# First MLP with ten pair groups and one plain group at its end, in place of eight and two

## The reference, cut to what matters

```python
# end of first_block
h = rms_norm(x, g_pre_mlp) * (1.0 + scale2) + shift2
f = jnp.square(jax.nn.relu(h @ w_fc1)) @ w_fc2        # 1024 -> 4096 -> 1024
x = x + gate2 * rms_norm(f, g_post_mlp)
# start of second_block
h = rmsnorm(x, attn_norm_g)
z = h @ w_in
```

## Time and profile before

| | |
|---|---|
| median of 3 runs | 2761.06 us (2756.93 to 2766.6) |
| the profiled execution | 2762.93 us; its span, first to last instruction, 2761.1 us |
| PE busy, share of the span | 97% |
| DVE, POOL, ACT busy | 66%, 46%, 38% |
| mean granted PE clock | 0.991 of full speed |

### The profile page before, as it was taken

How to read it: one execution, slowest core, us unless ns; L and a number is a source line. 1 busy time by engine, 2 the same in 40 slices (tenths; PEclk the granted TensorE clock), 3 DMA queues, 4 the chain that set the end, 5 groups by cost and what they waited for, 6 DMA issues and landing times.

```text
span 2761.1 us, 36980 instructions
## 1 busy us (share of the span) xinstructions
PE 2688.5 (97%) x14232; PEld 2146.1 (78%) x14232; DVE 1830.9 (66%) x2487; ACT 1042.8 (38%) x1705; POOL 1260.5 (46%) x774
## 2 busy tenths in 40 slices
PE   7999999999999999999999999999999999999998
PEld 4888888788888878886888566666887788888877
DVE  4853324657777776565999843798567677777763
ACT  5001114434444433455221456655114344444433
POOL 1433323454777754452232114010334677777773
PEclk9999999999999999999999999999999999999999
DMA  8541114343211224344133200000431112221123
GB/s 324 162 143 39 39 39 130 100 154 98 66 58 55 68 62 145 99 137 112 46 97 98 61 1 1 2 2 3 175 114 42 58 55 65 64 69 58 55 66 108
DMA packets 252697, 225.78 MB, mean 82 GB/s; under 512 B 24667, under 2 KB 220778, under 8 KB 252266
## 3 DMA queue, kind: packets, MB, share of 16 engines
q1 hardware_dynamic: 249498, 215.02, 25.0%
q10 hardware_dynamic: 3024, 8.39, 0.8%
HBM read 197.16 MB, written 25.17 MB: 81 GB/s over the span
## 4 chain that ended last, share of the span: by engine, by line
PE 85%; DVE 7%; ACT 3%; issue 3%; POOL 2%; DMA 0%; SPq 0%; ACTq 0%; DVEq 0%; POOLq 0%
PE PS L1479 21%; PE PS L1709 11%; PE PS L2075 9%; PE PS L2109 8%; PE PS L1758 5%; PE PS L1725 5%; PE PS L1775 5%; PE PS L2016 3%; PE PS L1463 3%; PE PS L1921 2%; PE PS L1983 2%; PE PS L2149 1%; DVE STEP L3852 1%; PE PS L1952 1%; PE PS L1891 1%
## 5 line engine op out<-in xcount | busy, mean ns | idle before, releaser
L1122 POOL TENSOR_TENSOR WLO<-RAW,WHI 128x1024 fp32r<-128x1024 f32 x113 | 272.8, 2414 | 471.9 <-ACT WHI L2259 471.8
L1109 POOL TENSOR_TENSOR WHI<-RAW,ZERO 128x1024 fp32r<-128x1024 f32 x46 | 91.5, 1989 | 494.0 <-PE PS L1479 238.2
L2259 ACT ACTIVATE WHI<-RAW 128x1024 fp32r<-128x1024 f32 x114 | 120.8, 1060 | 413.5 <-PE PS L1479 147.6
L1479 PE MATMUL PS<-H,WHI 128*128 128x512 f32 x864 | 271.1, 395 | 2.3 <-ACT CX L2187 1.2
L1479 PE MATMUL PS<-L,WHI 128*128 128x512 f32 x864 | 267.4, 391 | 0.0
L1479 PE MATMUL PS<-H,WLO 128*128 128x512 f32 x864 | 267.0, 390 | 0.0
L4063 DVE TENSOR_TENSOR X<-X,PS 128x1024 f32<-128x1024 f32 x182 | 214.6, 1213 | 4.9 <-PE PS L2109 3.3
L1336 POOL TENSOR_TENSOR QLO<-QRAW,QHI 128x512 fp32r<-128x512 f32 x116 | 171.7, 1481 | 80.9 <-ACT QHI L2724 80.7
L1709 PE MATMUL PS<-H,WHI 128*128 128x512 f32 x496 | 196.5, 396 | 1.4 <-DVE WLO L3344 0.6
L1709 PE MATMUL PS<-H,WLO 128*128 128x512 f32 x496 | 193.7, 391 | 0.0
L1709 PE MATMUL PS<-L,WHI 128*128 128x512 f32 x496 | 193.7, 390 | 0.0
(11 more groups left out here) (535 smaller groups left out, 6637.3 us busy)
## 6 DMA issues: line engine op xcount, KB each, us to landing
RAW<-w_fc SPq DMA_DIRECT2D x64, 512.0 KB, 4.0
RAW<-w_in SPq DMA_DIRECT2D x62, 512.0 KB, 3.8
DOWNRAW<-w_ff SPq DMA_DIRECT2D x81, 256.0 KB, 2.6
ADA<-w_ada SPq DMA_DIRECT2D x32, 512.0 KB, 5.3
QRAW<-w_ff SPq DMA_DIRECT2D x32, 512.0 KB, 4.0
RAW<-w_out SPq DMA_DIRECT2D x24, 512.0 KB, 3.8
DOWNRAW<-w_fc SPq DMA_DIRECT2D x40, 256.0 KB, 2.6
ADA_FIRST<-w_ada SPq DMA_DIRECT2D x16, 512.0 KB, 9.7
```

The source lines that it names most:

```text
L1122: nc.gpsimd.tensor_sub(WLO[w % 2][:, :], RAW[w % 2][:, :], WHI[w % 2][:, :].bitcast(F32)).then_inc(s_w, 1)
L1479: last = mm(bank(b + t), wt[:, k, :], half(a, (k + at) % KC, t), start=(k == 0 and n == 0), stop=(k == KC - 1 and n == 2))
```

## The change

`TAIL` becomes 1: ten pair groups, and then two blocks (group 7, half 0) and (group 7, half 1). The tiles of these blocks are called T0 to T15 from here on, T0 to T7 being the first block; T16 is the first tile of the projection. Around this:

- `back_sum` moves from the down tiles to the up tiles of the first block. ACT's copy for `back_sum(i)` stands at the end of ACT's step for the same tile i; it stood one step later than DVE's sum.
- Chain 2 runs beside the second block alone. Its stage 0 sums and spread stay ahead of the same matmuls (in T9), its stage 1 sums and spread move from the tenth tile of the chain to its seventh, T14, ahead of the second and sixth eighth of the tile.
- On DVE the order is written anew: the reciprocal of stage 0 behind the multiply and the low part of the first up tile, updates and accumulations in turn, the norms between the last two `half_sum`s.
- On ACT the squares of chain 2 are taken two for each tile from T10 to T13, the stage 1 root behind T13's, `H` behind T14 and T15, and all squares of `Y` for chain 3 behind T15.
- POOL writes its four chunks of `L` behind `WLO` of T16.
- The residual comes back in two parts: chunks 4 to 7 behind the `RAW` of T4, chunks 0 to 3 behind the `RAW` of T8.

```diff
--- before.py
+++ after.py
@@ -494,7 +494,7 @@
                     KC, 2 * KC, KC, KC)
         assert M1.w % 2 == 0
 
-        HEAD, TAIL = 2, 2
+        HEAD, TAIL = 2, 1
         BLOCKS1 = [(g, e) for e in range(2) for g in range(HEAD)]
         BLOCKS2 = [(g, e) for e in range(2) for g in range(GROUPS - TAIL, GROUPS)]
 
@@ -863,13 +863,15 @@
 
                             sp.wait_ge(c_xn, KC + k + 1)
                             sp.dma_start(xs[:, k * S:(k + 1) * S], chunk(X, k)).then_inc(s_xs, 16)
-                        k = 8 * n + i - 11
-                        if w0 == M1T.w and 0 <= k < KC:
-
-                            if k == 0:
+                        if w0 == M1T.w and 8 * n + i in (4, 8):
+
+                            if n == 0:
+                                sp.wait_ge(f_mm, done1(up_unit1(NG1 - 1, 2)))
+                                sp.wait_ge(s_xs, 16 + 16 * KC)
+                            else:
                                 sp.wait_ge(e_lo, TOKEN1_AT["back", 3])
-                                sp.wait_ge(s_xs, 16 + 16 * KC)
-                            sp.dma_start(chunk(X, k), xs[:, k * S:(k + 1) * S]).then_inc(s_xr, 16)
+                            for k in range(0 if n else 4, 4 if n else KC):
+                                sp.dma_start(chunk(X, k), xs[:, k * S:(k + 1) * S]).then_inc(s_xr, 16)
                         if w0 == M1.w and n == 2 and i == 0:
 
                             sp.wait_ge(c_lod, KC)
@@ -1260,16 +1262,15 @@
             down_sum1(g, 2)
             for n in range(4, 7):
                 down_low1(g, n)
-            for t in range(32):
-                if t == 29:
-                    chain_lows(2, 0)
-                if t == 30:
-                    chain_lows(2, 2)
+            for t in range(16 * TAIL):
                 low_part(M1T.w + t)
             for i in range(len(Z_TILES)):
                 if i == Z_OPEN:
                     chain_lows(3, 0)
                 low_part(Z0 + i)
+                if i == 0:
+                    chain_lows(2, 0)
+                    chain_lows(2, 2)
                 if i == Z_OPEN:
                     chain_lows(3, 2)
                 if i == Z_INDEX + 1:
@@ -1689,6 +1690,11 @@
                         chain_sums(q, 1)
                     if p == 5 and k == 6:
                         chain_spread(q, 1)
+                elif q == 2:
+                    if p == 6 and k == 1:
+                        chain_sums(q, 1)
+                    if p == 6 and k == 5:
+                        chain_spread(q, 1)
                 else:
                     if p == 9 and k == 2:
                         chain_sums(q, 1)
@@ -1782,13 +1788,13 @@
                 for n, (g, e) in enumerate(blocks):
                     for i in range(8):
                         t = 8 * n + i
-                        p = t - 16 * (q % 2 == 0)
+                        p = t - 8 * (m is M1T)
                         chain = q if 0 <= p < 16 else None
                         if i < 4:
                             ready = chain_ready(q - 1 + e) if i == 0 and n % 2 == 0 and m is M1 else None
                             if m is M1T and n == 0 and i == 1:
                                 pe.wait_ge(f_add, added1(NG1 - 1, 6) + 2)
-                            if m is M1T and n == 2 and i == 0:
+                            if m is M1T and n == 1 and i == 0:
                                 pe.wait_ge(e_lo, TOKEN1_AT["back", 3])
                             half_up(m.w + t, e, (H, L), ready, chain, p)
                         else:
@@ -2507,22 +2513,33 @@
                 act.wait_ge(f_mm, done1(ALONE1 + 4 + 2 * t))
                 high_part(M1T.w + t)
 
+            def sums_squared(n, columns):
+
+                for c in columns:
+                    act.wait_ge(*reads(M1T.w + 8 * n + 4 + c))
+                    for k in (2 * c, 2 * c + 1):
+                        branch_squared(16 + KC * n + k, half(Y, k, n))
+
             def tail_act(n, i):
 
-                e = n // 2
-                if n % 2 == 1 and i >= 5:
-                    for c in range(i - 5, i - 4 if i < 7 else 4):
-                        act.wait_ge(*reads(M1T.w + 8 * n + 4 + c))
-                        for k in (2 * c, 2 * c + 1):
-                            branch_squared(16 + KC * e + k, half(Y, k, e))
-                if n >= 2:
-                    chain_act_long(2, 8 * (n - 2) + i)
-                if n == 1 and i == 7:
-                    chain_act_long(2, -1)
-                if 5 <= 8 * n + i < 9:
-                    token_sum_high("back", 8 * n + i - 5)
-
-            half_blocks(M1T, BLOCKS2, 0, 34, tail_act)
+                if n == 0 and i >= 5:
+                    sums_squared(n, range(i - 5, i - 4 if i < 7 else 4))
+                if n == 0 and i < 4:
+                    token_sum_high("back", i)
+                if n == 0 and i == 7:
+                    chain_root(2, 0)
+                if n and 2 <= i <= 5:
+                    chain_square(2, 2 * i - 4)
+                    chain_square(2, 2 * i - 3)
+                if n and i == 5:
+                    chain_root(2, 1)
+                if n and i >= 6:
+                    for k in range(4 * i - 24, 4 * i - 20):
+                        chain_high(2, k)
+                if n and i == 7:
+                    sums_squared(n, range(4))
+
+            half_blocks(M1T, BLOCKS2, 0, 16 * TAIL + 2, tail_act)
             chain_act_short(3, -1)
 
 
@@ -3323,14 +3340,14 @@
 
             def hidden_low(m, n, i):
 
-                e, u = n // 2, 4 * n + i
+                e, u = n // (HEAD if m is M1 else TAIL), 4 * n + i
                 dve.wait_ge(*reads(m.w + 8 * n + i))
                 dve.wait_ge(s_hi, m.hi + u + 1)
                 V.tensor_sub(half(FL, i, e), RL[i % 2][:, HALF:S], half(FH, i, e).bitcast(F32)).then_inc(s_lo, 1)
 
             def half_sum(m, n, c, first=False):
 
-                e, w = n // 2, m.w + 8 * n + 4 + c
+                e, w = n // (HEAD if m is M1 else TAIL), m.w + 8 * n + 4 + c
                 dst = chunk(Y, 2 * c, 2).rearrange("p (c s) -> p c s", c=2)[:, :, e * HALF:(e + 1) * HALF]
                 src = bank(w_bank(w), 2).rearrange("p (c s) -> p c s", c=2)
                 dve.wait_ge(s_mm, w + 1)
@@ -3558,10 +3575,10 @@
 
             def back_beside(i):
 
-                if i >= 4:
-                    if i > 4:
-                        back_low(i - 5)
-                    back_sum(i - 4)
+                if 1 <= i <= 4:
+                    back_low(i - 1)
+                if i < 4:
+                    back_sum(i)
 
             def twelve_begun1(g):
 
@@ -3689,11 +3706,33 @@
             for n in range(4, 7):
                 down_read1(g, n)
             dve.wait_ge(f_add, added1(g, 6) + 2)
-            plain_block(M1T, 0, beside=back_beside)
-            plain_block(M1T, 1, squares=16, beside=lambda i: back_low(3) if i == 0 else None)
+            plain_block(M1T, 0, squares=16, beside=back_beside)
             dve.wait_ge(s_xr, 32 * KC)
-            chain_long(2, M1T, 2, False)
-            plain_sums(M1T, 3, squares=24)
+            for i in range(4):
+                hidden_squared(M1T, 1, i)
+                hidden_low(M1T, 1, i)
+                if i == 0:
+                    chain_recip(2, 0)
+                chain_update(2, i)
+                if i:
+                    chain_added(2, i)
+            chain_update(2, 4)
+            chain_added(2, 4)
+            half_sum(M1T, 1, 0)
+            chain_update(2, 5)
+            chain_added(2, 5)
+            half_sum(M1T, 1, 1)
+            chain_update(2, 6)
+            chain_added(2, 6)
+            chain_update(2, 7)
+            chain_added(2, 7)
+            chain_recip(2, 1)
+            chain_norms(2, 0, 3)
+            half_sum(M1T, 1, 2)
+            chain_norms(2, 4, 8)
+            half_sum(M1T, 1, 3)
+            for k in range(KC):
+                branch_square(24 + k)
             chain_recip(3, 0)
             chain_steps(3, 0, 9)
             chain_recip(3, 1)
```

## The result

The changed kernel takes 2779.59 us (median of 5 runs, 2777.13 to 2782.22), the kernel before 2761.06 us (now of 5 runs, the same median): ratio 1.0068, 95% interval 1.0057 to 1.008. It is slower, as forecast, by 18.5 us where 13 were forecast, and just above the range. The profiled execution took 2781.57 us (span 2779.8), 18.6 more than that of before.

What follows compares the result with a forecast made beforehand. PE's queue was taken to bound the kernel: waits of 22.7 us less 11.5 gained, net +11.2, plus 1.5 for the clock, +12.7; 2774 us after adjusting from the profiled execution to the runs' median, range 2764 to 2779.

Steps and rivals of the forecast that it cites:

- what PE gains: Two blocks of 88.1 us go out of PE's queue, two pair groups of 76.6 us come in: gain 11.5 us.
- RS in T9: PE waits 2.4 us at the stage 0 spread, the reciprocal being queued behind T8's multiply and `FL`.
- XACC in T14: PE waits 8.6 us at the stage 1 sums for DVE's last accumulations; floor of the term 6.3.
- the five places in T16 and T17: DVE's norms, ACT's `H` and POOL's `L` come late; 0.4 to 0.5 us lost at each place, 2.2 together.
- the circle: T10 to T14: one chain 2 update and accumulation, over DVE and ACT, takes about 2.9 us with the semaphores.
- the fetches: Residual chunks go out four together, twice, with `RAW` of T5 and T9 queued behind: costed at nothing, from above 4 us.
- The forecast's other case: First block: if POOL does not hold DVE's adds, the same walk gives a net 2.8 us lower.
- the walk to +6.6: First block: `back_sum` ends about +6.6 us after ACT's `WHI` starts, from `FL`'s end at 4.08 plus 2.5.
- Rival 4: The fetches late as well: net +15 to +19 us, 2776 to 2780; chance 0.06.
- I take one, after the longest, 1.5: Clock term: one half-clock stretch, after the longest wait, costs PE 1.5 us, making the net +12.7.
- rival 3: Half clock after every long wait, four over 2 us: 11.2 + 6 = +17.2 us, 2778; chance 0.14.
- Rival 1: Volume decides, not order: chain 2 hides in the blocks, whole 11.5 us gained, 2749.6 us; chance 0.09.

Runs made afterwards that it cites:

- run 1: Changed kernel with ACT's copy for `back_sum` one step later, as before the change: 2772.22 us, ratio 1.005 to the kernel before.
- run 2: Changed kernel with the stage 0 reciprocal ahead of T8's multiply and low part on DVE: 2774.82 us, ratio 1.0057 to the kernel before.
- run 4: Changed kernel with chain 2's stage 1 sums and spread in T15 in place of T14: 2772.1 us, ratio 1.0053 to the kernel before.
- run 5: Changed kernel with the squares of the first four chunks of `Y` and their additions taken early: 2773.44 us, ratio 1.005 to the kernel before.
- run 3: Changed kernel with 72 unread filler matmuls in the waits of T4, T9, T14 and T17: 2768.32 us, ratio 1.0038 to the kernel before.
- run 6: Changed kernel with the four order edits of runs 1, 2, 4 and 5 together: 2760.25 us, ratio 1.0005 to the kernel before.
- run 7: Run 6 reordered further: DVE's updates and accumulations earlier, five ACT squares a tile earlier, stage 1 sums back in T14: 2757.89 us, ratio 0.9995.
- run 9: Run 7 with unread filler matmuls, 10 ahead of the sums in T14 and 7 ahead of those in T17: 2752.83 us, ratio 0.9975.
- run 8: The changed kernel itself, unedited, measured again beside runs 5, 6 and 7: 2777.41 us, ratio 1.0062 to the kernel before.
- run 10: Changed kernel with 36 unread filler matmuls in the XACC wait of T14 alone: 2774.36 us, ratio 1.0052 to the kernel before.

## Why the prediction was off in size

**Right: what PE gains.** The two pair groups took 76.9 us, forecast 76.6. The first block took 50.2 us, forecast 48 to 50; 1.6 of it is clock.

**Right: the waits.** Forecast and measured, in us: `WLO` for T4 1.5 and 1.05; `FL` in T4 3.6 and 3.26; RS in T9 2.4 and 2.23; `FL` in T12 0.7 and 0.84; XACC in T14 8.6 and 8.23; the five places in T16 and T17 2.2 and 1.1; YACC in T17 3.3 and 3.67. ACT's steps beside T1 to T3, forecast 6.6, 7.2 and 7.2 us apart, were 6.55, 7.15 and 7.11, each ending in the copy that waits for DVE:

```profile
1106.14 1.05 ACT L2265 ACTIVATE WHI<-RAW 128x1024 fp32r<-128x1024 f32 x1
...
1112.79 0.60 ACT L2375 ACTIVATE H<-PS 128x512 fp32r<-128x512 f32 x1 [4.45 <-DVE PS L3521]
1113.29 1.05 ACT L2265 ACTIVATE WHI<-RAW 128x1024 fp32r<-128x1024 f32 x1
```

Runs 1, 2, 4 and 5 each took one cause away and its wait went, wholly or by the part forecast from its place. In the circle two accumulations came 2.74 us apart, where 2.9 was taken.

**Right in part by luck: their sum.** Without the clock the forecast's net is +11.2, and the account gives 20.5 - 9.2 = 11.3. But the waits were 19.6 us where the forecast added up 21.8, and the restarts and short gaps about 3 where it had 0.9. Two errors of 2 us cancel. A restart costs more than the 0.1 that the forecast took: around the 3.26 us wait in T4 two matmuls start 3.65 us apart (1120.83 and 1124.48), which is 3.26 + 0.23 and 0.16 more, and the next one follows after 0.33 us in place of 0.23.

**Right: the fetches are hidden.** The eight took 4.5 to 8.2 us to land (4.5/6.5/8.2, against the earlier trace rows), longer than any before, and no wait of the stage names them. The adds of `back_sum` were not held by POOL in T1 to T3: they took 0.68 to 0.69 us, because `WLO` was over by then; `FL` took 1.72 to 1.77 beside it. So the port rule of the Trainium skill ("SBUF — State Buffer", "SBUF: two separate sides") agrees with `FL`, and had no part in the adds here. The forecast's other case, a net 2.8 us lower if the adds are not held, did not come with it: the walk to +6.6 had already taken them at 0.6 us apart, as not held. Rival 4 (2776 to 2780) holds the measured time by its number only, since the fetches delayed nothing.

**Wrong: the clock.** The step that failed is "I take one, after the longest, 1.5". It had two faults. The count: not one stretch but four, one behind each wait of over 2 us, which is rival 3's mechanism. The size: rival 3 priced each at 1.5, "from above 6 us", and so this bound was no bound. The stretch behind the 8.2 us wait cost 3.2 and that in T17 2.6, since the sums, and in T9 the spread, ran at the lower level as well, and up to 12 matmuls with them. Together 9.2 by the count, 8.7 by run 3. With 9.2 in the place of 1.5 the forecast's net would have been +20.4; the stage ended +20.5 us late, and 1.8 came back later.

It follows that the range's upper edge was drawn from the wrong row. The earlier trace rows show that the clock fell beside a stop of a third of a microsecond, which spoke for counting every long wait; the argument against it, a clock of 1.00 in this stage, came from blocks in which PE never waited over 0.5 us, and so had nothing to say of waits of 2 to 8. The trace before had more to say at that place than the forecast took from it. The clock fell at 527.7, ahead of the short stop (528.36 to 528.74), and just ahead of the fall PE had done the sums of a norm chain behind a wait of their own, the pattern of T14 and T17:

```profile
526.29 1.02 PE L1669 MATMUL PS<-SC,YACC 128*128 128x1 f32 x8 [0.49 <-DVE YACC L3227]
```

**Rival 1** (volume, not order) was wrong for the change as it is. Runs 6 and 7 do the same work in other orders and end at 1.0005 and 0.9995, run 9 with 17 filler matmuls at 0.9975, so the loss was a matter of order and clock; the whole gain of 11.5 us (0.9958) that rival 1 promised was reached by none.

## What to carry to other kernels

When a schedule opens waits like these in a dense stream of matmuls (2.2 us and more here, 1.3 and more ahead of a norm chain's sums), price each twice: its own length, and a stretch at half clock behind it, here 1.6 to 3.2 us each. The second price doesn't follow from the length alone: see the next section. Work out the end of each engine's step with what stands behind it in the queue; in this case that gave every wait to 0.5 us, from rows of other stages. When a long wait can't be removed, filler matmuls in it may be worth more than they cost (8.7 us here for four waits), but moving the cause comes first: order alone took 23 us off the stage (173.5 in run 8, 149.8 in run 7: 23.7; 22.5 from the first profile) and 19.5 off the median.

## What the runs showed of the hardware that was not expected

- A wait of 1.27 us ahead of the sums was enough for a stretch at half clock: in runs 5, 6 and 7, all three that had it. In all the profiled runs, the waits of 1.27 to 8.2 us ahead of the XACC and YACC sums had one behind them each time (17 of 17). The same sums with no wait ahead of them (at 1247.88 in the changed kernel) ran at full clock.
- A wait of 2.2 or 3.3 us ahead of other work didn't bring one each time: the 3.26 us in T4 did in the changed kernel, its repetition and runs 5 and 10, not in runs 2 and 4; the 2.2 us in T9 did in the changed kernel, its repetition and runs 1 and 5, not in runs 4 and 10. Why is open; no run was made on it. One execution's profile is thus no proof that a wait has no clock cost.
- A wait of 1.7 us among the 128x512 matmuls of the last pair group (1073.77 in the changed kernel, 996.91 before) had none in any of the 12 profiled executions, nor had the 1.05 us in T4 in the seven that have it.
- In the changed kernel the clock was still 1.00 inside the 3.26 us wait and fell 1.0 us after the work had begun again (at 1125.5); in the 8.2 us wait it fell inside, at 1190.3, 5.1 us after PE had stopped. In run 8 it fell inside the 3.27 us wait as well, at 1122.5, and the stretch was twice as long. So the moment of the fall isn't set by the wait alone.
